# Hybrid decoder step with a 32-expert MoE on one core: the fourth tile of an expert's give-back is issued ahead of the next expert's down-projection

## What is computed

```
h   = rms_norm(x1, norm2)
group  = argmax(h @ w_group + b_group)                 # one of 4
expert = top 2 of the 8 experts of that group          # by h @ w_router + b_router
gate   = softmax(top 2) * softmax(groups)[group]
y      = sum over the two experts e of gate_e * ((silu(h @ w1[e]) * (h @ w3[e])) @ w2[e])
out    = x1 + y                                        # 520 tokens x 1024
```

## Time and profile before

| | us |
|---|---|
| median of 3 executions (lowest to highest) | 1183.52 (1182.88 to 1184.49) |
| profiled execution, its own time | 1182.75 |
| span of the profiled execution, first to last instruction | 1181.0 |
| TensorE busy in the span | 1104.3 (94%) |
| VectorE busy | 523.8 (44%) |
| ScalarE busy | 326.2 (28%) |
| GpSimd busy | 130.0 (11%) |

### The profile page before, as it was taken

The page is one execution under the profiler, slowest core; times in us unless marked ns, Lnnn a source line. Parts: engine busy times, 40 slices in busy tenths (PEclk is TensorE's granted clock), DMA queues, the critical chain, the costliest instruction groups (busy, mean ns, idle before and its releaser), DMA issues.

```text
span 1181.0 us, 15790 instructions
## 1 busy us (share of the span) xinstructions
PE 1104.3 (94%) x6499; PEld 698.6 (59%) x6499; DVE 523.8 (44%) x733; ACT 326.2 (28%) x444; POOL 130.0 (11%) x179
## 2 busy tenths in 40 slices
PE   6999999999989999999998299999999999999996
PEld 5999977988667767799545233333333333333332
DVE  5222234886644333443122524444444555554445
ACT  5323211355368676633112011110011111111100
POOL 0000000013201322100000101111111111111110
PEclk9999899999989999999999589999999999999998
DMA  5622222554511322274414679999999999999941
GB/s 183 249 90 91 66 78 74 196 185 164 188 54 45 99 72 90 73 277 169 165 39 177 250 300 421 427 426 425 429 426 426 425 426 426 426 426 428 425 177 73
DMA packets 50067, 282.99 MB, mean 240 GB/s; under 512 B 6242, under 2 KB 6514, under 8 KB 29524
## 3 DMA queue, kind: packets, MB, share of 16 engines
q1 hardware_dynamic: 41188, 254.78, 53.7%
q0 software_dynamic: 6048, 20.98, 5.3%
q10 hardware_dynamic: 2768, 6.33, 1.5%
HBM read 274.56 MB, written 7.48 MB: 239 GB/s over the span
## 4 chain that ended last, share of the span: by engine, by line
PE 87%; DVE 6%; ACT 2%; DMA 2%; issue 1%; SPq 0%; DVEq 0%; POOL 0%; ACTq 0%; POOLq 0%
PE acc_all L746 25%; PE acc_all L1214 19%; PE acc_all L1228 10%; PE acc_all L876 5%; PE acc_all L1124 5%; PE acc_all L1239 5%; PE acc_all L725 4%; PE acc_all L807 2%; PE acc_all L988 2%; PE acc_all L1002 2%; PE acc_all L1242 2%; PE acc_all L1007 1%; PE acc_all L926 1%; DMA vals<-in_cache_mem_v 1%; DVE gate_h L2120 1%
## 5 line engine op out<-in xcount | busy, mean ns | idle before, releaser
L746 PE MATMUL acc_all<-xn_hi,w_hi 128*128 128x260 f32 x832 | 174.2, 291 | 10.6 <-DVE gate_sb L1822 6.0
L746 PE MATMUL acc_all<-xn_hi,w_lo 128*128 128x260 f32 x832 | 168.8, 285 | 0.0
L746 PE MATMUL acc_all<-xn_lo,w_hi 128*128 128x260 f32 x832 | 168.6, 285 | 0.0
L2131 DVE TENSOR_TENSOR x<-x,acc_all 128x1024 f32<-128x1024 f32 x128 | 152.6, 1215 | 1.8 <-PE acc_all L1239 0.9
L746 PEld LDWEIGHTS acc_all<-xn_hi,w_hi 128*128 128x128 f32 x832 | 130.2, 191 | 18.5 <-issue 17.1
L746 PEld LDWEIGHTS acc_all<-xn_lo,w_hi 128*128 128x128 f32 x832 | 129.9, 191 | 0.0
L746 PEld LDWEIGHTS acc_all<-xn_hi,w_lo 128*128 128x128 f32 x832 | 129.6, 190 | 0.0
L688 POOL TENSOR_SCALAR spread<-tok_row,slots 128x560 fp32r<-128x560 f32 x32 | 54.0, 1686 | 405.3 <-PE acc_all L1242 405.2
L1666 DVE TENSOR_TENSOR w_lo<-w_raw,w_hi 128x1024 fp32r<-128x1024 f32 x52 | 63.4, 1222 | 63.4 <-ACT w_hi L1353 63.2
L1597 ACT ACTIVATE gate_h<-acc_all 128x256 f32<-128x256 f32 x32 | 12.3, 383 | 260.3 <-PE acc_all L725 260.3
L2115 DVE COPY up_sb<-acc_all 128x512 f32<-128x512 f32 x32 | 22.1, 692 | 133.7 <-PE acc_all L1215 133.7
(11 more groups left out here) (355 smaller groups left out, 1886.2 us busy)
## 6 DMA issues: line engine op xcount, KB each, us to landing
w_a<-in_w SPq DMA_DIRECT2D x44, 1024.0 KB, 12.9
w_b<-in_w SPq DMA_DIRECT2D x44, 1024.0 KB, 13.2
w_c<-in_w SPq DMA_DIRECT2D x40, 1024.0 KB, 13.0
w_raw<-in_w_in SPq DMA_DIRECT2D x52, 512.0 KB, 3.6
w_a<-in_w SPq DMA_DIRECT2D x11, 2048.0 KB, 14.4
w_b<-in_w SPq DMA_DIRECT2D x11, 2048.0 KB, 13.9
w_c<-in_w SPq DMA_DIRECT2D x10, 2048.0 KB, 14.3
w_br<-in_w_branch SPq DMA_DIRECT2D x24, 256.0 KB, 4.4
```

The costliest lines, as they stand in the source:

```text
L746: mm = pe.matmul(out[:, a, :], w[:, slot, k, :], x[:, k, a * HALF_TOK:(a + 1) * HALF_TOK], start=first, stop=last)
L2131: dve.tensor_tensor(x1[:, t, :], x1[:, t, :], bank(2 * pair, 2), ALU.add).then_inc(back_ok, 1)
```

## The change

For experts 1 to 30, tile 3 of the expert before is issued behind tile 2, ahead of the wait for act_t and of down(n), where it stood behind down(n) before. VectorE's addition of tile 3 goes with it: it stands behind the addition of tile 2, ahead of y_rest_out, where it stood behind y_rest_out. Tile 4 stays where it was. In expert 31 the two lists of tiles are written differently and the order stays as it was. The counts that the waits use don't change.

```diff
@@ TensorE, for n in range(NE)
                 if n >= 1:
-                    give(n - 1, (2,))
+                    give(n - 1, (2, 3))
                 if n == NE - 1:
-                    give(n - 1, (3, 4))
+                    give(n - 1, (4,))
                 pe.wait_ge(actt_ok, n + 1)
                 if n >= 1:
                     pe.wait_ge(rest_ok, n)
                 down(n % WS, n // WS + 1)
                 if 1 <= n < NE - 1:
-                    give(n - 1, (3, 4))
+                    give(n - 1, (4,))
@@ VectorE, for n in range(NE)
                 act_out(n)
                 if n >= 1:
-                    added(n - 1, (1, 2) if n < NE - 1 else (1, 2, 3, 4))
+                    added(n - 1, (1, 2, 3) if n < NE - 1 else (1, 2, 3, 4))
                 dve.wait_ge(top_ok, n + 1)
                 y_rest_out(slot_gate[:, n:n + 1])
                 if 1 <= n < NE - 1:
-                    added(n - 1, (3, 4))
+                    added(n - 1, (4,))
```

## The result

The changed kernel takes 1217.84 us (median of 4, 1216.86 to 1219.54) against 1183.2 (median of 4, 1182.64 to 1184.49): the ratio is 1.0294, with a 95% interval of 1.0281 to 1.0307. It was run a second time beside the last experiments: 1217.01 us, ratio 1.0304 (1.0279 to 1.0328). It is slower, and by what the prediction gave (1217 us; 33.9 us more, against 34.1 us of span). The profiled execution took 1216.86 us with a span of 1215.1 us, 34.1 us over the earlier trace rows.

A forecast was written before the change was run, and what follows sets the result against it. TensorE in its written order was taken to set the pace, with DMA full but early. 30 experts at +1.13 us add 33.9 us to the profiled 1182.75, 1216.7, stated as 1217 us; range 1213 to 1234.

The forecast's parts named there:

- the sum: Whole kernel: 30 experts at +1.13 us each, 33.9 us on the profiled 1182.75 us.
- the term that decides: Tile 3 waits for tile 1's addition: +1.79 us ahead of the down-projection, -0.66 behind, +1.13 an expert.
- the price of the clock: Expert 31's down-projection: a clock drop costs 1.70 us; none more taken for the middle experts.
- The rival: Middle experts: new idle time lowers the clock often, 1234 us for one in three, 1268 for all; chance 0.15.
- row for "no drop": Before 1170.07 the clock stayed up through 1.67 us of idle time, so no middle-expert drop was taken.
- The predicted share of 0.95: DMA engines, middle experts: the longer period leaves spare time, so their busy share falls to about 0.95.
- The rival by which DMA sets the pace: Expert stage: weight loads govern the period and absorb TensorE's stall, 1183 or 1208 us; chance 0.03.
- The third rival: Ahead of the down-projection: tile 3 fills the wait for act_t, 8.3 us less, 1174 us; chance 0.01.

The follow-up runs named there:

- both tiles moved: Kernel before, with tiles 3 and 4 both ahead of the down-projection in every expert, VectorE's additions of tiles 1 to 4 ahead of y_rest_out: 1239.99 us, ratio 1.0477.
- the fastest version: Kernel before, with sample tile 4 through bank 5 ahead of the down-projection, not waiting for tile 1's addition, expert 31 in the same order: 1168.09 us, ratio 0.9878.

## Why the prediction was right

**The mechanism and the sum.** Every step of the term that decides came out as worked: tile 3's start 1.27 us behind the additions' start (919.14 - 917.87; predicted 1.27), the down-projection 0.66 behind it (919.80 - 919.14; 0.66), 0.66 saved behind (tile 4 at 923.39, 3.59 us behind the down-projection's start), 0.60 from tile 4 to the next up-projection (0.59). The period is 16.26 (16.25), and 30 x 1.13 = 33.9 stands against 34.1 us of span. The experiments bear out the cause: the wait without the move, as the first of the waits, gives the same idle time and period (16.46 and 16.34 in other places), TensorE's list alone gives the whole loss, VectorE's list alone none, the same tile with its bank free earlier costs 0.11 us an expert, and another tile with the same wait costs as much as tile 3, without it nothing.

**Expert 31 as a model.** It had the new order in the kernel before, and gave the 1.27 and the price of the clock. Its own idle time of 1.54 us was not the one to take over: the middle experts turn the next pair's tokens ahead of tile 2, which then starts later, and have 1.41.

**VectorE, tile 4, ScalarE, GpSimd.** Costed at nothing, rightly: y_rest waits 3.53 us for y_top (3.52 before), and VectorE's list alone changes nothing.

**The clock.** Taken as no further drop in a middle expert, and up to expert 29 there was none. In expert 30 there was one, which the sum did not have: the last period of 17.87 us gives 17.87 - 16.25 = 1.62 us for it, predicted 1.70. Expert 31's own drop failed to come (a short one followed in its last matmuls instead, granted 0.50 from 1207.30 to 1209.50). That the two cancelled, and the sum held to 0.2 us, is luck. The rival got 0.15. The prediction's reason, that expert 31 waits more than once and a middle expert only once, fits what was seen: one idle time of 1.41 to 1.61 us lowered no middle expert's clock in this kernel, with TensorE's list alone, with the wait alone in its three places, or with the sample tile and the wait, while two idle times (0.24 and 1.55 us in expert 30, 1.41 and 0.39 us with both tiles moved) did. But it is no rule. Expert 31 kept its clock here with the idle times under which it fell before, so did two of three experts with both tiles moved, expert 30 kept it with the wait alone, and in the fastest version the clock fell at the end of the kernel after one idle time of 1.72 us (before 1155.43; granted 0.53 from 1155.00 to 1166.00), hardly more than the 1.67 us that the prediction leant on. Its row for "no drop" was weaker than it took it to be.

**DMA.** The predicted share of 0.95 did not show: it stayed at 1.00 while the rate fell from 426 to 403 GB/s. This step failed, the reading of that share as a measure of the load, and no term of the sum hung on it; the landing times carried the argument rightly, growing before and level after. The rival by which DMA sets the pace is refuted from both sides, by the loss here and by the gain of 14 us at a period of 14.78.

**Faster.** The third rival asked for tile 1's addition before 902.9. Placed ahead of act_t by hand, it ended at 903.16 in the time of the earlier trace rows (900.81 + 2.35), past the 902.9 asked for, so tile 3 still waited 0.26 us, and act_t, now second on VectorE, came 0.77 us later. The period was 15.23 us, no gain. The gain that was in the gap came from a tile that waits for no addition.

## What to carry to other kernels

Before a piece of work is moved into a wait, look up what the piece itself waits for, and whether the engine that frees its buffer does so before or after it produces what the first wait is for: on an in-order engine the new wait then holds everything behind it, here 1.41 us for a gap of 0.28. If one end of the loop already has the new order, its rows give the price, but its idle times differ where it has less work (1.54 us here, 1.41 in the middle). A filler pays when its buffer is free at that moment; a small piece through an idle bank did what the large piece could not.

## What the runs showed of the hardware that was not expected

- The same stall costs differently by the place of its wait among waits that are long met: periods of 16.25, 16.46 and 16.34 us with the stalling wait first, third and last of four ahead of the same matmul. Two guesses at it fell, and the cause is open.
- The DMA engines' busy share over 700 to 1130 us was 1.01 at 426 GB/s, 1.00 at 403 and 0.96 at 383 (both tiles moved). It did not tell a queue that falls behind from one that keeps up; the time from issue to landing did (level at 10 us in the changed kernel, 11.5 to 18.5 before, 11.7 to 26.5 in the fastest version).
- The granted clock stayed at 1.00 through a single 1.41 us of idle time in experts 1 to 29 of the changed kernel. It fell in expert 30, where 0.24 us of idle time came ahead of the 1.55 us, and in every third expert from expert 3 on once 0.39 us followed the 1.41 us a tile later. The same idle times did not always lower it: not in two of three experts with both tiles moved, and in expert 31 before the change but not after it. A drop cost 1.50 to 1.62 us where it was read.
